# Turning the attention weights of two attentions one step later

## The reference

```
s = (q @ k.T) * scale + bias          # first layer: a bias by distance; second: the forget sums
p = masked_softmax(s, key_pos <= t)   # 256 queries, 256 keys, causal
o = p @ v                             # in the first layer p is multiplied by a gate as well
```

## Time and profile before

| what | value |
|---|---|
| median of 3 runs | 1283.28 us (1282.92 to 1283.64) |
| the profiled execution's own time | 1284.39 us |
| its span, first to last instruction | 1282.6 us |
| mean granted TensorE clock | 0.982 of full |
| busy: PE, DVE, ACT, POOL | 1209.8, 826.6, 653.9, 242.0 us |
| first attention, first turn to the next stage | 102.50 to 147.86 us |
| second attention, first scores to the next stage | 424.42 to 458.18 us |

### The profile page before, as it was taken

One profiled execution on the slowest core, in us unless ns is written; L12 is line 12 of the kernel. 1 busy time (PEld: TensorE's weight loads), 2 busy tenths in 40 slices (PEclk: granted clock), 3 DMA queues, 4 the chain that ended last, 5 costly groups with the idle time before them and its releaser, 6 DMA issues.

```text
span 1282.6 us, 19213 instructions
## 1 busy us (share of the span) xinstructions
PE 1209.8 (94%) x7770; PEld 1055.8 (82%) x7770; DVE 826.6 (64%) x1275; ACT 653.9 (51%) x1060; POOL 242.0 (19%) x316
## 2 busy tenths in 40 slices
PE   6898899999999889999999999999998689999996
PEld 5785688888888578888888889999985479888996
DVE  6955586666586567666657776468754656776643
ACT  6436566644343656664446555355535444655531
POOL 4104331110000331120112221000005501112101
PEclk9999999999999999999999999999999879999998
DMA  7780145555454235556544555544440024455461
GB/s 272 269 204 34 55 176 197 179 216 194 143 191 185 112 113 183 189 176 225 184 178 154 187 187 175 185 165 165 164 140 20 1 80 159 164 197 178 154 205 56
DMA packets 34088, 205.56 MB, mean 160 GB/s; under 512 B 3776, under 2 KB 6352, under 8 KB 13776
## 3 DMA queue, kind: packets, MB, share of 16 engines
q1 hardware_dynamic: 30704, 200.47, 44.1%
q10 hardware_dynamic: 3296, 3.87, 1.5%
HBM read 202.87 MB, written 1.46 MB: 159 GB/s over the span
## 4 chain that ended last, share of the span: by engine, by line
PE 79%; DVE 13%; ACT 3%; POOL 3%; issue 1%; DMA 0%; POOLq 0%; ACTq 0%; DVEq 0%
PE ps L662 35%; PE ps L667 23%; PE ps L665 5%; PE ps L666 5%; DVE wl L604 4%; POOL pb L965 2%; PE ps L686 1%; PE ps L688 1%; PE ps L687 1%; DVE tf L2172 1%; PE ps L909 1%; ACT wh L575 1%; DVE y L1932 1%; PE ps L1420 1%; PE ps L2444 1%
## 5 line engine op out<-in xcount | busy, mean ns | idle before, releaser
L604 DVE TENSOR_TENSOR wl<-raw,wh 128x2048 fp32r<-128x2048 f32 (+4 forms) x196 | 421.3, 2154 | 150.1 <-ACT wh L575 150.0
L662 PE MATMUL ps<-xb,wh 128*128 128x512 f32 x1424 | 502.1, 398 | 5.0 <-DVE wl L604 3.9
L667 PE MATMUL ps<-xb,wl 128*128 128x256 f32 x1696 | 476.0, 281 | 0.0
L575 ACT ACTIVATE wh<-raw 128x2048 fp32r<-128x2048 f32 (+4 forms) x196 | 348.6, 1781 | 152.0 <-PE ps L667 118.6
L662 PEld LDWEIGHTS ps<-xb,wh 128*128 128x128 f32 x1424 | 267.3, 188 | 71.4 <-issue 5.6
L667 PEld LDWEIGHTS ps<-xb,wl 128*128 128x128 f32 x1696 | 321.4, 190 | 0.0
L667 PE MATMUL ps<-ab,wl 128*128 128x256 f32 x1088 | 307.7, 283 | 0.0
L662 PE MATMUL ps<-ab,wh 128*128 128x512 f32 x640 | 226.8, 399 | 0.8 <-DVE ab L975 0.8
L667 PEld LDWEIGHTS ps<-ab,wl 128*128 128x128 f32 x1088 | 208.1, 191 | 0.0
L662 PEld LDWEIGHTS ps<-ab,wh 128*128 128x128 f32 x640 | 120.2, 188 | 31.6 <-DVE ab L975 1.4
L859 DVE TENSOR_TENSOR tf<-ps,tf 128x256 f32<-128x256 f32 x148 | 62.0, 422 | 119.6 <-ACT tf L854 119.6
(11 more groups left out here) (322 smaller groups left out, 1376.3 us busy)
## 6 DMA issues: line engine op xcount, KB each, us to landing
raw<-wstream SPq DMA_DIRECT2D x156, 1024.0 KB, 4.8
raw<-wstream SPq DMA_DIRECT2D x32, 704.0 KB, 4.1
raw<-wstream SPq DMA_DIRECT2D x8, 768.0 KB, 4.2
e_bt<-scratch ACTq DMA_DIRECT2D x16, 128.0 KB, 8.8
o_bt<-scratch SPq DMA_DIRECT2D x2, 1024.0 KB, 10.0
raw<-wstream SPq DMA_DIRECT2D x2, 560.0 KB, 8.0
raw<-wstream SPq DMA_DIRECT2D x4, 256.0 KB, 6.5
h<-xt ACTq DMA_DIRECT2D x4, 256.0 KB, 7.7
```

The lines of the kernel that those rows point to most:

```text
L575: e.g.activation(WH[i % HLN][:, 0:w], RAW[i % RAWN][:, 0:w], ACT.Copy).then_inc(S["hi"], 1)
L604: e.g.tensor_tensor(WL[q][:, 0:w], RAW[i % RAWN][:, 0:w], f32(WH[q][:, 0:w]), ALU.subtract).then_inc(S["lo"], 1)
L662: e.g.matmul(PS[b][:, :].rearrange("p (a t) -> p a t", a=2), wh[:, sl], x2[:, :, cs], start=start, stop=k == p.nk - 1, skip_group_check=pair)
L667: ins = e.g.matmul(o, wl[:, sl], xh[:, cs], start=False, stop=k == p.nk - 1, skip_group_check=pair)
```

## The change

In both attentions the turn of head i is made at step i+3 instead of i+2, on PE. The copies, the value products and the outputs that hang on it move by one step too, and since copies, value products and outputs go by pairs, what stood in an even step stands in an odd one now and the other way round. All loops get one step more. The turn of the compressed map and its copies move from step 11 to 12. Scores, minimum, exponential, reciprocal, weighting and the quarters keep their steps, and nothing is added or left out. After it, PE does in step i: scores of heads i+1 and i+2 (odd i), the turn of head i-3, the value products of heads i-5 and i-4 (odd i).

The diff:

```
--- before.py
+++ after.py
@@ -1134,7 +1134,7 @@
                 e.wait_ge(S["pcx"], tb + 1)
                 e.g.activation(pcv[:, tb, :, 0:15], pcv[:, tb, :, 0:15], ACT.Exp).then_inc(S["pce"], 1)
             A = EVEN
-            for i in range(A.n + 3):
+            for i in range(A.n + 4):
                 if i == 2:
                     act_exp_biased(e, A, 2)
                     act_exp_biased(e, A, 3)
@@ -1147,11 +1147,11 @@
                     hi_part(e, G["eo"].first + i // 12, i % 6)
                 if i < A.n and i not in (2, 3):
                     act_exp_biased(e, A, i)
-                if 0 <= i - 2 < A.n and i % 2 == 0:
-                    act_turned(e, A, i - 2)
-                if 0 <= i - 3 < A.n and even_last(i - 3):
-                    d = even_pair(i - 3)
-                    act_out(e, d, PS[even_bank(d)][:, 0:256], i - 3 + 1, d)
+                if 0 <= i - 3 < A.n and i % 2:
+                    act_turned(e, A, i - 3)
+                if 0 <= i - 4 < A.n and even_last(i - 4):
+                    d = even_pair(i - 4)
+                    act_out(e, d, PS[even_bank(d)][:, 0:256], i - 4 + 1, d)
             act_gemm(e, G["eo"], drain=act_residual(S["h_eo"], 1))
 
         def even_pair(i):
@@ -1262,14 +1262,14 @@
                                   nmx[:, tb * 8:tb * 8 + 8].unsqueeze(2).broadcast_to([128, 8, 15]),
                                   ALU.subtract).then_inc(S["pcx"], 1)
             A = EVEN
-            for i in range(A.n + 4):
+            for i in range(A.n + 5):
                 if i == 2:
                     dve_gemm(e, G["ev1"], 0, ahead=0)
                 if i in (7, 9):
                     dve_even_gates(e, i // 9)
                 if 10 <= i < 14 or 16 <= i < 20:
                     lo_part(e, G["eo"].first + i // 16, (i - 10) % 6)
-                if i == 11:
+                if i == 12:
                     e.wait_ge(S["pcm"], 1)
                     e.g.tensor_copy(e_ptc[0][:, :], PS[0][:, 0:256])
                     e.g.tensor_copy(e_ptc[1][:, :], PS[0][:, 256:512]).then_inc(S["ptc"], 1)
@@ -1279,10 +1279,10 @@
                     dve_max_biased(e, A, i, e_bt[:, h * 256 + 128:h * 256 + 256], e_bt[:, h * 256:h * 256 + 256])
                 if 0 <= i - 1 < A.n:
                     dve_reciprocal(e, A, i - 1)
-                if 0 <= i - 2 < A.n and i % 2:
-                    dve_turned(e, A, i - 2)
-                if 0 <= i - 4 < A.n and even_last(i - 4):
-                    d = even_pair(i - 4)
+                if 0 <= i - 3 < A.n and i % 2 == 0:
+                    dve_turned(e, A, i - 3)
+                if 0 <= i - 5 < A.n and even_last(i - 5):
+                    d = even_pair(i - 5)
                     dve_out(e, d, PS[even_bank(d)][:, 0:256], d)
             dve_gemm(e, G["eo"], 1, drain=dve_residual(G["eo"], S["h_eo"], 1), between=behind_chunk(1))
 
@@ -1392,12 +1392,12 @@
                     ins.then_inc(S["pcm"], 1)
                 if i % 2 and i + 1 < A.n:
                     pe_even_scores(e, i + 1)
-                if 0 <= i - 2 < A.n:
-                    if i - 2 < 2:
-                        e.wait(G["even"].free.get(A.turn_bank(i - 2)))
-                    pe_turn(e, A, i - 2)
-                if i % 2 == 0 and 0 <= i - 4 < A.n:
-                    pe_even_pv(e, i - 4)
+                if 0 <= i - 3 < A.n:
+                    if i - 3 < 2:
+                        e.wait(G["even"].free.get(A.turn_bank(i - 3)))
+                    pe_turn(e, A, i - 3)
+                if i % 2 and 0 <= i - 5 < A.n:
+                    pe_even_pv(e, i - 5)
             pe_cols(e, G["eo"], range(8), AB, o_ready(0))
 
         def pe_even_scores(e, i):
@@ -1624,14 +1624,14 @@
             act_gemm(e, G["ov0"], drain=act_toks(G["ov0"], o_v, 0, 2))
             act_gemm(e, G["ov1"], drain=act_toks(G["ov1"], o_v, 512, 2), ahead=0)
             A = ODD
-            for i in range(A.n + 3):
+            for i in range(A.n + 4):
                 if 2 <= i < 10:
                     hi_part(e, G["oo"].first + (i - 2) // 4, (i - 2) % 4)
                 if i < A.n:
                     act_exp_biased(e, A, i)
-                if 0 <= i - 2 < A.n and i % 2 == 0:
-                    act_turned(e, A, i - 2)
-                q = i - 3
+                if 0 <= i - 3 < A.n and i % 2:
+                    act_turned(e, A, i - 3)
+                q = i - 4
                 if 0 <= q < A.n and q % 2 == 1:
                     act_out(e, q // 2, PS[q // 2 % 2][:, 0:256], A.base + q + 1, 8 + q // 2)
             act_gemm(e, G["oo"], drain=act_residual(S["h_oo"], 3))
@@ -1661,9 +1661,9 @@
                     dve_max_biased(e, A, i, o_bt[i // 8][:, at:at + 128], o_bt[i // 8][:, at:at + T])
                 if 0 <= i - 1 < A.n:
                     dve_reciprocal(e, A, i - 1)
-                if 0 <= i - 2 < A.n and i % 2:
-                    dve_turned(e, A, i - 2)
-                q = i - 4
+                if 0 <= i - 3 < A.n and i % 2 == 0:
+                    dve_turned(e, A, i - 3)
+                q = i - 5
                 if 0 <= q < A.n and q % 2 == 1:
                     dve_out(e, q // 2, PS[q // 2 % 2][:, 0:256], 8 + q // 2)
             dve_gemm(e, G["oo"], 1, drain=dve_residual(G["oo"], S["h_oo"], 3), between=behind_chunk(3))
@@ -1683,15 +1683,15 @@
             pe_toks(e, G["ov1"], x_ready(2))
             A = ODD
             pe_odd_scores(e, 0)
-            for i in range(A.n + 3):
+            for i in range(A.n + 4):
                 if i % 2 and i + 1 < A.n:
                     pe_odd_scores(e, i + 1)
-                if 0 <= i - 2 < A.n:
-                    if i - 2 < 2:
-                        e.wait(G["odd"].free.get(A.turn_bank(i - 2)))
-                    pe_turn(e, A, i - 2)
-                q = i - 4
-                if i % 2 == 0 and 0 <= q < A.n:
+                if 0 <= i - 3 < A.n:
+                    if i - 3 < 2:
+                        e.wait(G["odd"].free.get(A.turn_bank(i - 3)))
+                    pe_turn(e, A, i - 3)
+                q = i - 5
+                if i % 2 and 0 <= q < A.n:
                     d = q // 2
                     b = d % 2
                     if d < 2:
```

## The result

The changed kernel took 1272.28 us in the median of 6 runs (1268.36 to 1277.12), beside 1283.1 for 6 runs of the kernel before: ratio 0.9921, 95% interval 0.9898 to 0.9945. Its profiled execution took 1273.46 us with a span of 1271.6.

The account below looks back on a forecast made before the run. PE's weight products fill most of the kernel; in the attentions a ring through VectorE's queue makes PE wait. Gains of 7.0 and 3.4 us, together 10.4, off 1283.28 gave 1272.9 us; own range 1271.0 to 1274.5, with the clock case 1270.8 to 1276.6.

Parts of the forecast that it names:

- The ring through VectorE's queue: Second attention: odd head's copy stands ahead of the minimum and reciprocal its next turn needs; 4.04 us per two heads.
- Head 16: 124.05: First attention: head 16's minimum starts at 124.05 against 129.08, some 1.6 us of it from the clock.
- (c): ScalarE's copy and output move from even to odd steps, behind the odd exponential.
- (d): First attention: gate transposes and their two copies move from step 11 to 12; cost the same in both orders.
- the replay: Each engine's queue re-timed in its new order, each start the latest of its predecessors; gave 7.0 and 3.4 us.
- 3.4 and 2.7: Second attention after head 10: the next two pairs, set by VectorE, against 4.04 and 3.44.
- a pair of 2.9 us: First attention, heads 16 to 23: PE bounds the pairs, mean 2.9 us against 3.8.
- part (b): VectorE's odd copy moves to the next even step, with 3.1 us of other work covering 1.9 us of weighting and turn.
- The slow clock: Rival: slow clock stays in the first attention or comes elsewhere; costs 1.6 to 3.2 us, 1274.5 to 1276.1; chance 0.15.
- PE ran ahead: Opposite of the rival that PE doesn't run ahead: pairs 4.02 us, 1 us won in all, 1282.3; chance 0.05.
- The buffer of four: Rival: a head's minimum waits for a later turn through buffer reuse; 4.3 us slower, 1287.6; chance 0.02.
- 0 to 1 us in all: Bound on the cost of GpSimd's weighting running more beside VectorE, 1.20 rather than 0.83 us a head.

Follow-up runs that it names:

- e6: Kernel before plus one small extra GpSimd operation ahead of every head's weighting in both attentions; 1286.54 us, second attention 36.09 us.
- e8: Kernel before with only VectorE's subtraction for the low output one step later, in the second attention alone; 1282.98 us, that attention 31.67 us.
- e7: Kernel after plus one small extra GpSimd operation ahead of every head's weighting in both attentions; 1268.64 us.
- e3: Kernel after with PE's turns and ScalarE's copies back in their old steps, VectorE's copies, value products and outputs still late; 1278.32 us, ratio 0.9977.
- e4: Kernel after with ScalarE's copy of the turned even head ahead of the same step's exponential, both attentions; 1273.24 us, ratio 0.9934.
- the second comparison: Kernels before and after, both unchanged, run again; medians 1282.23 us (12 runs) and 1273.92 us (7 runs), ratio 0.9943.
- e1: Kernel before with the change in the first attention alone; 1276.3 us, ratio 0.9967.
- b1: Kernel before, unchanged, run again for a second trace; median 1282.23 us over 12 runs.
- a1: Kernel after, unchanged, run again for a second trace; 1273.92 us, ratio 0.9943.
- e2: Kernel before with the change in the second attention alone; 1278.15 us, ratio 0.9986.
- e5: Kernel after with only VectorE's copies of the odd heads back in their old step; first attention 44.45 us, second 1.54 us shorter than before.
- e9: The same kernel as e4, run again with more rounds; 1271.71 us, ratio 0.9925.

## Why the prediction was right, and where its sizes were off

**The ring through VectorE's queue, opened.** Right. It was what bounded the second attention (e6, e8), and the new order takes weighting and turn out of the chain (e7). In the first attention PE's queue was a second bound, which e3 shows; I had named it only from head 16 on.

**First attention: 7.0 us predicted, 5.46 measured.** In times from the last product ahead, the minimum of head 4 came at 1.77 us (predicted 1.58, before 3.27), that of head 12 at 16.44 (16.28). The term mis-sized is "Head 16: 124.05": from head 12 to 16 it took 6.88 us, not 6.15. e4 needs 6.53 us for this stretch, so 0.35 of these 0.73 us is ScalarE's copy standing behind the exponential, with PE's even turn waiting for the shared buffer; the rest no run separates. (e4 reaches head 16 0.60 us earlier than the kernel after, but 0.25 of that by head 12.) I had written of parts (c) and (d) "Their cost is the same in both orders": for (c) that is the sentence that failed. From head 16 to 23 another 0.36 was missing and in the drain 0.25, which makes the 1.5 us. The clock was 1.45 us of the gain where I took 1.6, and at equal clock the order gave 4.0 where I had 5.4.

**Second attention: 3.4 us predicted, 2.58 measured.** Up to the exponential of head 10 the replay holds: 2.23 us won, predicted 2.2. Then "3.4 and 2.7" were in fact 3.61 and 3.30. VectorE was in time: it reached the minimum of head 12 in 3.31 us and that of head 14 in 2.72. But ScalarE was late. Its timeline, kernel after:

```profile
441.82 0.40 ACT L916 ACTIVATE pb<-pb,nm 128x128 f32<-128x128 f32 x1 [0.80 <-DVE nm L927]
...
442.72 0.47 ACT L935 ACTIVATE pt<-ps 128x384 f32<-128x384 f32 x1
443.09 0.37 ACT L971 ACTIVATE ab<-ps 128x256 fp32r<-128x256 f32 x1
443.35 0.39 ACT L916 ACTIVATE pb<-pb,nm 128x128 f32<-128x128 f32 x1
```

The exponential of head 13 waits 0.80 for its minimum, and then copy and output, 0.63, stand ahead of that of head 14. From head 14 to 15 0.3 came back, and the drain was 0.59 longer than before instead of 0.29: the missing 0.8 is 0.5 up to the last exponential and 0.3 behind it. e4 recovers 0.27 in all, so here the copy is the smaller part. What remains up to the last exponential goes with a wait of VectorE, of which my replay has nothing: with the quarters over, the reciprocal of head 13 comes due before ScalarE has that head's exponential, and the minimum of head 15 stands behind it. (VectorE's waits for exponentials are 4.0 us in this attention after the change, 2.2 before.) Timeline of DVE, kernel after:

```profile
442.84 0.17 DVE L959 RECIPROCAL rs<-sm 128x2 f32<-128x2 f32 x1 [0.43 <-ACT pb L917]
```

That is read off the trace and no experiment separates it, nor the longer drain.

**The total.** 1272.9 us was predicted from 10.4 us in the attentions; they gave 8.0, and by the second comparison the kernels are 8.3 us apart. From the same 1283.28 us the measured 8.0 would have given 1275.2. That the first median came out at 1272.28 is owed to stages which the change doesn't touch, and was luck.

**Two slips in the working.** For heads 16 to 23 it sets a pair of 2.9 us "against 3.8"; the rows give 11.46 us for seven heads, 3.3 a pair. The sum was taken from the rows and isn't touched by it. And the "3.1 us of other work" of part (b) adds up to 3.19, or 3.27 with the second reciprocal that stands there too, which makes the ring only more open.

**The rivals.** The slow clock went, as forecast, but from an order that shows it in three traces of four, so that the change keeps it away is likely and not shown. The Trainium skill ("TensorE: Matmul & The Clock Gate", Part 4) says that turns do not count as busy for the clock in the way products do; by that rule a slow stretch could have stayed, and the five traces with the whole change in the first attention have none. As both orders have the same turns, no run here tests the rule itself. PE ran ahead (copies 3.31 us apart, not 4.02). The buffer of four did not bind: with the ring open the pairs take 3.31 to 3.72, and in the second attention VectorE waits for no turn at a minimum.

**The bounds.** "0 to 1 us in all" for a slower weighting holds: e7 put 0.24 us or more, start to start, ahead of each head's weighting, and the two attentions together were not longer (70.16 us, after 70.26).

## What to carry to other kernels

On an in-order engine ask of each piece that waits on a round trip through others what stands behind it and starts the next round; a 0.34 us operation moved behind that start took 0.27 us off every round, 1.40 us in an attention. After a ring is opened, price the next queue on the path, and above all who still holds the buffer that the moved piece writes. When executions scatter more than the effect, compare stretches of the trace, which here repeat to some hundredths at equal clock, and sum those; count each from the same instruction.

## What the runs showed of the hardware

**Two rates of the same stage.** In the second gate stage a chunk takes 5.65 us in the traces of before, e1, e3, e4 and e7 and 5.55 in those of after, b1, a1, e2, e5, e6, e8 and e9, whatever the order of the attentions; all stages but the attentions together took 1197 to 1204 us over the thirteen traces. What chooses the rate I don't know.

**The clock.** In the old order it fell to the lower level at 121 in before and b1, after a stretch in which PE stood for part of the time, and not in e2. What PE did ahead of it was the same: counted from the attention's start, VectorE's minima of heads 4 to 13 begin within 0.01 us of each other in b1 and e2, and PE's busy time is the same in the same ten microseconds of each. Table of stretches of b1, then of e2:

```profile
110.58:120.58 10.00, 6.44 (x52) 3.92 (x52) 9.38 (x43) 8.10 (x30) 4.98 (x10) 1.00 0.01 3
109.37:119.37 10.00, 6.44 (x52) 3.92 (x52) 9.38 (x43) 8.11 (x30) 4.98 (x10) 1.00 0.01 3
```

So the same work in this stage can bring the fall or not; what decides, these runs don't show. Its cost is seen by comparing the two: 1.45 us. Stretches at the lower level were there too in e5 (two in the first attention) and e6 (three, and one in the second attention). In e7 the granted clock is recorded as 0.95 nearly throughout, and it was not slower for it: its attentions are those above, and its other stages took 1196.6 us together, the least of the thirteen.

**VectorE beside GpSimd.** The weighting of a head takes 0.83 us by itself in the second attention and 1.20 to 1.30 beside VectorE's work, and VectorE's quarter 0.71 to 0.78 beside it instead of 0.67: what the new order hides it also stretches. e6 shows it for one small operation: 0.27 us by itself, 0.63 where it begins together with a quarter. Timeline of GpSimd in e6, an odd head and the even one behind it, then VectorE's quarter:

```profile
440.39 0.62 POOL L966 TENSOR_SCALAR slow<-consts 128x92 f32<-128x92 f32 x1 [1.77 <-DVE rs L960]
...
441.79 0.26 POOL L966 TENSOR_SCALAR slow<-consts 128x92 f32<-128x92 f32 x1
```

```profile
440.22 0.67 DVE L594 TENSOR_TENSOR wl<-raw,wh 128x512 fp32r<-128x512 f32 x1
```

The Trainium skill ("SBUF — State Buffer", "Who interferes with whom") says that a VectorE instruction with two SBUF inputs and a GpSimd instruction that reads SBUF exclude each other. The quarter has two such inputs, and these rows agree, as far as one operation can show it: GpSimd's, begun at 440.39, ends 0.12 us behind the quarter's end at 440.89.
